# Rows of the last norm: 256-column bank, squares shared by two engines, gain multiplied in ahead

## The reference

```python
def rms_norm(x, gain):
    xf = x.astype(jnp.float32)
    xf = xf * lax.rsqrt(jnp.mean(xf * xf, axis=-1, keepdims=True) + EPS)
    return (xf * gain.astype(jnp.float32)).astype(x.dtype)

def second_block(x, norm_gain, ..., w_out, final_gain):
    h = x
    for l in range(DEPTH):
        h = hybrid_layer(h, ..., norm_gain[l], ..., w_out[l])   # rms_norm first, h + y @ w_out last
    return rms_norm(h, final_gain)
```

## Time and profile before

| | us |
|---|---|
| median of three runs | 1179.17 (1177.88 to 1179.58) |
| the profiled execution, its own time | 1179.37 |
| its span, first to last instruction | 1177.5 |
| TensorE matmul busy | 1160.3 (99%) |
| VectorE busy | 741.8 (63%) |
| ScalarE busy | 570.4 (48%) |
| GpSimd busy | 26.2 (2%) |
| mean granted TensorE clock | 0.998 |

### The profile page before, as it was taken

How to read it: one execution, slowest core, us unless ns; L and a number is a source line. 1 busy time by engine, 2 the same in 40 slices (tenths; PEclk the granted TensorE clock), 3 DMA queues, 4 the chain that set the end, 5 groups by cost and what they waited for, 6 DMA issues and landing times.

```text
span 1177.5 us, 18016 instructions
## 1 busy us (share of the span) xinstructions
PE 1160.3 (99%) x7546; PEld 1042.4 (89%) x7546; DVE 741.8 (63%) x994; ACT 570.4 (48%) x658; POOL 26.2 (2%) x36
## 2 busy tenths in 40 slices
PE   8999999999999999999999999999999899999997
PEld 6988998998999988998998898899988689978995
DVE  5877556667655546686764667755545666775674
ACT  5563445442544434454444534444432556845673
POOL 0000000001000000000000000000000000000000
PEclk9999999999999999999999999999999999999999
DMA  9664454556665563745545556665566363336420
GB/s 343 220 215 144 144 181 176 180 186 201 224 212 190 167 212 112 250 151 172 170 144 189 179 179 214 230 208 182 169 203 208 125 215 128 127 138 243 137 80 36
DMA packets 129871, 211.45 MB, mean 180 GB/s; under 512 B 6528, under 2 KB 52608, under 8 KB 129664
## 3 DMA queue, kind: packets, MB, share of 16 engines
q1 hardware_dynamic: 128048, 204.02, 51.9%
q0 software_dynamic: 1744, 6.29, 1.8%
HBM read 209.24 MB, written 1.05 MB: 179 GB/s over the span
## 4 chain that ended last, share of the span: by engine, by line
PE 89%; DVE 5%; ACT 3%; DMA 2%; issue 1%; SPq 0%; POOL 0%; DVEq 0%; POOLq 0%; ACTq 0%
PE ps L463 85%; DMA raw<-in_w_in 2%; DVE wl L1362 1%; ACT wh L937 1%; PE ps L656 1%; PE ps L691 1%; PE ps L794 0%; DVE mqk L1490 0%; PE ps L596 0%; ACT sg L1100 0%; ACT xh L973 0%; DVE sg L1642 0%; PE ps L776 0%; PE ps L663 0%; DVE yl L1832 0%
## 5 line engine op out<-in xcount | busy, mean ns | idle before, releaser
L1362 DVE TENSOR_TENSOR wl<-raw,wh 128x2048 fp32r<-128x2048 f32 (+1 forms) x190 | 424.0, 2237 | 180.0 <-ACT wh L937 179.6
L937 ACT ACTIVATE wh<-raw 128x2048 fp32r<-128x2048 f32 (+1 forms) x190 | 359.9, 1900 | 181.0 <-PE ps L463 166.1
L463 PE MATMUL ps<-xh,wh 128*128 128x256 f32 x1200 | 337.1, 282 | 0.0
L463 PE MATMUL ps<-xl,wh 128*128 128x256 f32 x1200 | 332.1, 277 | 0.0
L463 PE MATMUL ps<-xh,wl 128*128 128x256 f32 x1184 | 328.4, 277 | 0.0
L463 PEld LDWEIGHTS ps<-xh,wh 128*128 128x128 f32 x1200 | 225.9, 188 | 3.2 <-issue 2.4
L463 PEld LDWEIGHTS ps<-xl,wh 128*128 128x128 f32 x1200 | 226.0, 188 | 0.4
L463 PEld LDWEIGHTS ps<-xh,wl 128*128 128x128 f32 x1184 | 222.6, 188 | 0.0
L463 PE MATMUL ps<-wh,xh 128*128 128x512 f32 (+1 forms) x512 | 203.8, 398 | 4.7 <-DVE wl L1362 2.4
L463 PE MATMUL ps<-wh,xl 128*128 128x512 f32 (+1 forms) x512 | 196.9, 385 | 0.0
L463 PE MATMUL ps<-wl,xh 128*128 128x512 f32 (+1 forms) x512 | 196.7, 384 | 0.0
(11 more groups left out here) (259 smaller groups left out, 1384.6 us busy)
## 6 DMA issues: line engine op xcount, KB each, us to landing
raw<-in_w_in SPq DMA_DIRECT2D x90, 1024.0 KB, 5.1
raw<-in_w_gate_up SPq DMA_DIRECT2D x88, 512.0 KB, 4.9
raw<-in_w_down SPq DMA_DIRECT2D x20, 1024.0 KB, 4.9
raw<-in_w_out SPq DMA_DIRECT2D x16, 1024.0 KB, 5.0
raw<-in_w_proj_ret SPq DMA_DIRECT2D x8, 1024.0 KB, 4.9
raw<-in_w_proj_mlstm SPq DMA_DIRECT2D x8, 1024.0 KB, 5.0
rows<-in_ln_g POOLq DMA_DIRECT2D x4, 512.0 KB, 4.3
rows<-in_ln_b POOLq DMA_DIRECT2D x4, 512.0 KB, 5.7
```

What stands on the lines that cost most here:

```text
L463: return pe.matmul(o, a, b, start=start, stop=False, skip_group_check=True)
L937: act.activation(stretch(wh, u, 0, m), source(u)[:, 0:m], ACT.Copy).then_inc(s_hi, 1)
L1362: dve.tensor_tensor(stretch(wl, u, a, nk * n), source(u)[:, a:nk * n], f32(stretch(wh, u, a, nk * n)), ALU.subtract).then_inc(s_lo, 1 if a ...
```

## The change

Four edits. (1) In the norm's sums ACT squares only the columns 0 to 511, now with the factor 1/D inside; DVE squares the columns 512 to 1023 in one instruction that multiplies, scales, sums and starts from epsilon (`square_sum`, a tensor_tensor_reduce). The separate scaling (L1638) goes. This holds for all three norms. (2) For the last row tile of the last layer, c = 1 is computed in two halves of 256 columns: the first in its own bank, the second in an aux bank with the new name `2e`. (3) In that tile TensorE does k = 4 to 7 for all of c = 0, then for the first 256 columns of c = 1, then for the rest. (4) DVE treats that tile in its own order (`last_rows`): the gain is multiplied into the columns 0 to 767 before the norm's value is known; ACT multiplies the columns 0 to 511 by that value, DVE the others. SP's third store waits for a new semaphore `s_last`.

```diff
@@ sync
-                    sp.wait_ge(s_rm, 4 * 2 + 2 * t + c + 1)
+                    if t == 1 and c == 0:
+                        sp.wait_ge(s_last, 2)
+                    else:
+                        sp.wait_ge(s_rm, 4 * 2 + 2 * t + c + (t == 0))
@@ tensor, project, first part (k = 0 to 3)
-                            r = tok3(bank[t][:, :], yh, yl, k, t, h_[:, k, :], l_[:, k, :], k == 0)
+                            if end_of_all(l, t) and c == 1:
+                                if k == 0:
+                                    rest, _ = open_aux("2e", l)
+                                tok3(bank[t][:, 0:256], yh, yl, k, t, h_[:, k, 0:256], l_[:, k, 0:256], k == 0)
+                                r = tok3(rest[:, 0:256], yh, yl, k, t, h_[:, k, 256:512], l_[:, k, 256:512], k == 0)
+                            else:
+                                r = tok3(bank[t][:, :], yh, yl, k, t, h_[:, k, :], l_[:, k, :], k == 0)
@@ tensor, project, second part
                 for t in range(2):
+                    if end_of_all(l, t):
+                        ends = (0, 0, 512, main("o0", l)[1], s_used), (1, 0, 256, main("o1", l)[1], s_used), (1, 256, 512, *aux("2e", l)[:2])
+                        for c, a, z, o, full in ends:
+                            u, nk, h_, l_ = last[c]
+                            for k in range(4, 8):
+                                r = tok3(o[:, 0:z - a], yh, yl, k, t, h_[:, k - 4, a:z], l_[:, k - 4, a:z], False)
+                            r.then_inc(full, 1)
+                        continue
@@ scalar
-            def squares(t, v, waits):
-                for c in range(2):
-                    act.wait_ge(*waits[c])
-                    r = act.activation(xn(t)[:, col_half(c)], X[:, t, col_half(c)], ACT.Square, accum_out=st6[:, t, c, 0:1])
-                r.then_inc(s_sq, 1)
+            def squares(t, ready, value, rest):
+                act.wait_ge(ready, value)
+                act.activation(rest, X[:, t, 0:512], ACT.Square, scale=D ** -0.5, accum_out=st6[:, t, 0, 0:1]).then_inc(s_sq, 1)
@@ scalar, at the end
+                    squares(t, free, v + 1, flat(xc) if end_of_all(l, t) else xn(t)[:, 0:512])
+                    if end_of_all(l, t):
+                        act.wait_ge(s_last, 1)
+                        act.wait_ge(s_rms, 6)
+                        act.activation(xn(t)[:, 0:512], xn(t)[:, 0:512], ACT.Copy, scale=rsd[:, t:t + 1]).then_inc(s_last, 1)
@@ vector
-            def mean_square(t, n):
+            def square_sum(x_, start_, sum_):
+                return dve.tensor_tensor_reduce(x_[0], x_[1], x_[1], 1.0 / D, start_, ALU.mult, ALU.add, sum_)
+
+            def mean_square(t, n, x_ready):
+                x_ready()
+                after(own(square_sum((xn(t)[:, 512:1024], X[:, t, 512:1024]), RMS_EPS, rsd[:, t:t + 1])))
                 dve.wait_ge(s_sq, n)
-                after(own(dve.tensor_tensor(rsd[:, t:t + 1], st6[:, t, 0, 0:1], st6[:, t, 1, 0:1], ALU.add)))
-                dve.tensor_scalar(rsd[:, t:t + 1], rsd[:, t:t + 1], 1.0 / D, RMS_EPS, ALU.mult, ALU.add).then_inc(s_ms, 1)
+                dve.tensor_tensor(rsd[:, t:t + 1], st6[:, t, 0, 0:1], rsd[:, t:t + 1], ALU.add).then_inc(s_ms, 1)
@@ vector, new function for the last tile
+            def last_rows(l):
+                o, x_, gain, bank = xn(1), X[:, 1, :], rows2, main("o1", l)[1]
+                residual(l, "o0", 1, 0, 1.0)
+                main_done("o0", l, 1)
+                dve.wait_ge(s_row2, 48)
+                dve.tensor_tensor(o[:, 0:512], x_[:, 0:512], gain[:, 0:512], ALU.mult).then_inc(s_last, 1)
+                main_full("o1", l, 1)
+                after(own(dve.tensor_tensor(x_[:, 512:768], x_[:, 512:768], bank[:, 0:256], ALU.add)))
+                n = own(square_sum((o[:, 768:1024], x_[:, 512:768]), RMS_EPS, rsd[:, 1:2]))
+                own(dve.tensor_tensor(o[:, 512:768], x_[:, 512:768], gain[:, 512:768], ALU.mult))
+                after(n)
+                dve.wait_ge(s_sq, 6)
+                own(dve.tensor_tensor(st6[:, 1, 1, 0:1], st6[:, 1, 0, 0:1], rsd[:, 1:2], ALU.add))
+                rest, _ = aux_full("2e", l)
+                after(own(dve.tensor_tensor(x_[:, 768:1024], x_[:, 768:1024], rest[:, 0:256], ALU.add)))
+                square_sum((o[:, 768:1024], x_[:, 768:1024]), st6[:, 1, 1, 0:1], rsd[:, 1:2]).then_inc(s_ms, 1)
+                dve.wait_ge(s_rms, 6)
+                dve.tensor_scalar(o[:, 512:768], o[:, 512:768], rsd[:, 1:2], None, ALU.mult)
+                dve.scalar_tensor_tensor(out=o[:, 768:1024], in0=x_[:, 768:1024], scalar=rsd[:, 1:2], in1=gain[:, 768:1024],
+                                         op0=ALU.mult, op1=ALU.mult).then_inc(s_rm, 1)
```

More of the change, by code:

```diff
@@ L146 @@
         "V2", "c0", "c1", "T6", "T7", "c2", "c3", "V3", "l0", "l1", "k0", "k1", "k2", "k3", "p0", "p1",
-        "x00", "x01", "x10", "x11")
+        "x00", "x01", "x10", "x11", "e")
 SIDE1 = {
@@ L203, in tables @@
         for name in AUX2:
-            if (l, name[0]) != (1, "x"):
+            if (l, name[0]) not in ((1, "x"), (0, "e")):
                 aux["2" + name, l], n = n, n + 1
@@ L294, in program @@
         s_drain = [sem(f"s_drain{i}") for i in range(4)]
-        s_cst, s_par, s_x, s_warm, s_gw, s_row, s_row2, s_out = (
-            sem(n) for n in ("s_cst", "s_par", "s_x", "s_warm", "s_gw", "s_row", "s_row2", "s_out"))
+        s_cst, s_par, s_x, s_warm, s_gw, s_row, s_row2, s_out, s_last = (
+            sem(n) for n in ("s_cst", "s_par", "s_x", "s_warm", "s_gw", "s_row", "s_row2", "s_out", "s_last"))
         s_xT = [sem(f"s_xT{q}") for q in range(3)]
@@ L322, in program @@
         f32 = lambda ap: ap.bitcast(F32)
+        end_of_all = lambda l, t: l == DEPTH - 1 and t == 1
         flat = lambda a: a[:, :, :].rearrange("p k t -> p (k t)")
@@ L1179, in scalar @@
                 else:
-                    by_half("dn1", l, 3, 3, lambda t: squares(t, 4, [(s_xn, 12 + 2 * t + c + 1) for c in range(2)]),
+                    by_half("dn1", l, 3, 3, lambda t: squares(t, s_xn, 12 + 2 * t + 1, xn(t)[:, 0:512]),
                             lambda: split_x("xb", l, 0, 4))
@@ L1337, in scalar @@
                         highs(use + RING)
-                    waits = [(freed(f"o{c}", l, t)[0], freed(f"o{c}", l, t)[1] + 1) for c in range(2)]
-                    squares(t, 5 + l, waits)
+                    free, v = freed("o0", l, t)
+                    squares(t, free, v + 1, flat(xc) if end_of_all(l, t) else xn(t)[:, 0:512])
[3 more added lines that the diff above has]
+                        act.activation(xn(t)[:, 0:512], xn(t)[:, 0:512], ACT.Copy, scale=rsd[:, t:t + 1]).then_inc(s_last, 1)
         def vector(dve):
@@ L1661, in normal @@
                 if n == 4:
-                    mean_square(t, t + 1)
+                    mean_square(t, t + 1, lambda: dve.wait_ge(s_xn, 12 + 2 * t + 2))
             def first_ff(l, j, t):
@@ L1940, in vector @@
                         raise_high(use + RING)
+                    if end_of_all(l, t):
+                        last_rows(l)
+                        continue
                     for c in range(2):
@@ L1944, in vector @@
                         first_half_low()
-                    mean_square(t, 2 * l + 2 + t + 1)
+                    mean_square(t, 2 * l + 2 + t + 1, lambda: main_done(f"o1", l, t))
         block = top.enter_context(nc.Block())
```

## The result

The changed kernel runs in 1177.52 us in the median of 21 runs (1176.08 to 1178.98), the kernel before, in 21 runs taken beside them, in 1179.17 (1177.88 to 1181.72). The ratio is 0.9987, with a 95% interval of 0.9981 to 0.9993: 0.8 to 2.2 us less. It is faster, by less than the 0.2% that the prediction named as what one such measurement tells from no change. The forecast was 1178.4. The profiled execution took 1178.22 us, with a span of 1176.4.

A forecast was written before the change was run, and what follows sets the result against it. TensorE was taken as the bound, so only places where it waits, and the end, count. End 0.16, norms 1 and 2 0.44 and norm 4 0.39 sum to 0.99: 1179.37 - 0.99 = 1178.4 us, range 1177.8 to 1179.0, outer 1176.7 to 1180.0.

The forecast's parts named there:

- The bound at the end: Last rows: DVE alone sets the end, reaching the first 512 columns a whole microsecond after their bank filled.
- The norm's sum of the last rows: End of the kernel: the last square-and-sum ends at 1172.85 instead of 1172.97, gain 0.12 us.
- The end as a whole: Last stores: the second lands at 1176.99 instead of 1177.15, gain 0.16 us.
- the four 256-column steps: Last rows on DVE: these dependent steps eat nearly all that the earlier start wins.
- Square-and-sum: DVE's new instruction in the norms: priced at 0.69 us for 512 columns, 0.42 for 256.
- ACT's scaled copy: Last rows: ACT scales the first half, a copy with a scale per row, taken as 0.7 us.
- Norms 1 and 2: Down-projection's end in layer 1: DVE squares the second half itself, 0.22 us earlier each, 0.44 together.
- Norm 4: Output projection of layer 0, second rows: sum 0.80 earlier, of which PE's 0.39 us wait is the gain.
- Rival 2: Square-and-sum runs at half rate with two SBUF sources: 2.1 us back, 1180.5 us; chance 0.08.
- Rival 3: Earlier gains don't arrive because PE meets another hidden wait; only the end remains: 1179.2 us; chance 0.12.
- Rival 1: Shorter PE waits around 928.57 keep the granted clock up: 1.46 us more gained, 1176.9 us; chance 0.17.

The follow-up runs named there:

- norms_only: Changed kernel with the new sums in all norms, but the last rows' rework undone: median 1177.09 us, ratio 0.9988.
- busy_before: Kernel before, plus five unused 512-column matmuls on TensorE while it waits for norm 2's products: median 1178.25 us, ratio 0.9992.
- old_order: Changed kernel with the last rows' matmuls put back into the old order: 1181.76 us in one run.
- end_only: Changed kernel with norms 1 to 5 summing as before, only the last rows reworked: median 1178.47 us, ratio 1.0000.

## Why the prediction was right

**The bound at the end** was read rightly: DVE reached the first 512 columns 1.0 us after TensorE had delivered them (forecast 1.0) and had no idle time from there to its last sum, and the last bank was full 0.7 us before DVE took it (forecast 0.7). The norm's sum of the last rows earlier by 0.12: measured 7.26 - 7.16 = 0.10. The end as a whole, 0.16: measured 0.15, in a length that scatters by 0.06. That the four 256-column steps eat into what the earlier start wins was right, "nearly all" was too much: the sums alone bring 0.20 (7.26 to 7.06, norms_only), and the split takes 0.10 of it back. What I had not seen is that the rework adds nothing at all to the end: with the last rows left as before it is just as short (11.64).

**Prices.** Square-and-sum 0.69 for 512 columns: 0.69. For 256, 0.42: 0.43, but 0.48 where its start value is a column in memory, which I had left out. ACT's scaled copy 0.7: 0.72; no row of before had it, and by the Trainium skill's formula (page "ScalarE: Activation LUTs", section "What ACT_TABLE_LOAD costs") it was 0.71. Here the trace agrees.

**Norms 1 and 2**, 0.44: A shrank by 0.41. **Norm 4**, 0.39: B shrank by 0.39, and PE's weight loads have no wait left. Together with the end 0.95 against 0.99 forecast. The cleanest check is D in two profiles without the fall: busy_before 266.98, the changed kernel 266.04, 0.94 apart.

**Rival 2**, half rate with two SBUF sources, is refuted: 0.69 and 0.43 with both sources in SBUF. The rule of the Trainium skill's page "Vector Engine (DVE) Microarchitecture Reference" (section "Points that are easy to get wrong") does not show in this operation here; the measurement decides. **Rival 3** did not occur: what norms 1, 2 and 4 won arrives at the end, since D without the fall shrank by 0.94, and A, B and C together by 0.95.

**Rival 1**, the clock, is the one thing that the forecast weighed wrongly. Its price was right (1.46 forecast; 1.40 between the two profiles, 1.48 between the two groups of runs of before). But I treated the fall as something that a kernel has or has not, to be kept or lost by the change, with 0.17 for losing it. It comes in some executions and not in others: the profile of the changed kernel hasn't it, that of old_order, with the same code there, has. So the 1178.4, worked out from an execution with the fall, stood for one kind of execution and was compared with a median over both kinds.

How much of the miss that explains is not shown. The measured medians lie 1.65 apart and not 0.99, and taking 0.99 from the median 1179.17 instead of from the profiled 1179.37 gives 1178.2, still 0.7 above the measured 1177.52. A smaller share of falls in the changed kernel would account for it, and so would chance: the ratio's interval (0.8 to 2.2 us) holds 0.99. That 1177.52 lies inside the forecast's outer range is in part owed to that width, which covers rival 1 as well; what the experiments bear out is 0.95 of the 0.99 that the steps were to bring.

## What to carry to other kernels

In a serial tail, write down each engine's queue from the last handover on, with what it waits for: then one sees who is late, and that an operand that arrives earlier for an engine that is late already wins nothing. Moving half of a reduction to the engine that waits for it anyway won everything here (0.95 us); splitting the last bank for finer overlap put 0.1 us of extra steps on DVE, the late engine, and won nothing. Before a sum is made against a profiled execution, compare its span with those of all runs, and say whether it holds an event, such as a fall of the clock, that others lack. And compare two kernels by a length within the profile that starts where the change starts: here the spans of two profiles differed by 1.1 us, near the 0.95 of the steps only by coincidence, since a start 1.26 later and a missing fall of 1.40 nearly cancelled.

## What the runs showed of the hardware that was not expected

POOL's power on 128x1 took 0.93 us in place of 0.54 while DVE ran a product with two SBUF inputs beside it, and 0.54 again without. The Trainium skill's page "SBUF — State Buffer" (section "Who interferes with whom") says that such an instruction contends with a GpSimd instruction that reads SBUF; the trace agrees, at 0.39 us. Read again, the profiles had it all along, before the change too (1.00 at 911.03, 0.55 at 914.81): in the changed kernel the layer norm's power, beside DVE's products (L1699), takes 1.00 us, the next one, beside nothing, 0.54.

```profile
912.29 1.00 POOL L422 TENSOR_TENSOR small<-small,cst 128x1 f32<-128x1 f32 x1 [167.86 <-DVE small L1695]
915.86 0.54 POOL L422 TENSOR_TENSOR small<-small,cst 128x1 f32<-128x1 f32 x1 [2.57 <-DVE small L1662]
```

TensorE's clock fell near 930 us in some profiled executions and not in others that run the same code there: 3.4 us at 0.50, that is 1.2 GHz, in the kernel before (929.9 to 933.4), at a price of 1.4 to 1.5 us. The first 110 us of the program, up to POOL's first power, differ by up to 2.8 us between profiles (109.27 in end_only, 112.03 in old_order), and old_order's granted clock is at 0.83 and 0.75 in 32 to 40 us, where that of before is at 1.00:

```profile
32.00:36.00 4.00, 2.10 (x13) 1.95 (x12) 2.69 (x5) 2.05 (x4) 0.00 (x0) 0.83 0.77 269
36.00:40.00 4.00, 4.00 (x29) 4.00 (x29) 3.18 (x20) 3.75 (x3) 0.00 (x0) 0.75 0.80 262
```
